# Where ScalarE makes the gate rows of four tokens: one block of eight per group, or two blocks of four in neighbouring places

## The reference, cut to what matters

```python
idx = i1 * PEER_KEYS + i2
gate = jax.nn.softmax(best_s, axis=-1).astype(x.dtype)
...
hid = jnp.einsum('td,tkd->tk', xb, u[ib])
act = jax.nn.gelu(hid, approximate=False) * gb
return jnp.einsum('tk,tkd->td', act, v[ib])
```

## Time and profile before

| | |
|---|---|
| median of 3 runs | 3329.31 us (3320.22 to 3340.08) |
| the profiled execution | 3332.39 us |
| its span, first to last instruction | 3330.6 us |
| TensorE busy with matmuls, share of the span | 99% |
| VectorE, ScalarE, GpSimd busy | 83%, 60%, 14% |
| mean granted clock of TensorE | 0.995 |

### The profile page before, as it was taken

How to read it: one execution, slowest core, us unless ns; L and a number is a source line. 1 busy time by engine, 2 the same in 40 slices (tenths; PEclk the granted TensorE clock), 3 DMA queues, 4 the chain that set the end, 5 groups by cost and what they waited for, 6 DMA issues and landing times. The chain is left out here.

```text
span 3330.6 us, 52168 instructions
## 1 busy us (share of the span) xinstructions
PE 3287.9 (99%) x19468; PEld 2943.0 (88%) x19468; DVE 2780.6 (83%) x4033; ACT 1992.6 (60%) x3618; POOL 482.5 (14%) x262
## 2 busy tenths in 40 slices
PE   9999999999999999999999999999999999999998
PEld 8888879999999988888878887999999998888887
DVE  5775569999988878888987757999898888888988
ACT  4444555555888855555555545555688875555555
POOL 0000000011222211223210000011122211122330
PEclk9999999999999999999999999999999999999999
DMA  7553345798999989999984344578899999999996
GB/s 271 179 185 131 113 160 191 257 347 317 360 360 363 366 336 351 359 360 383 377 307 153 119 152 157 201 285 334 316 377 363 364 341 350 359 354 365 375 378 225
DMA packets 169221, 969.07 MB, mean 291 GB/s; under 512 B 18912, under 2 KB 52704, under 8 KB 55648
## 3 DMA queue, kind: packets, MB, share of 16 engines
q1 hardware_dynamic: 132192, 698.61, 55.7%
q0 software_dynamic: 36864, 268.45, 21.5%
HBM read 951.26 MB, written 15.73 MB: 290 GB/s over the span
## 5 line engine op out<-in xcount | busy, mean ns | idle before, releaser
L1688 DVE TENSOR_TENSOR wl<-raw,wh 128x1024 fp32r<-128x1024 f32 x1264 | 1522.8, 1219 | 421.1 <-ACT wh L580 416.2
L580 ACT ACTIVATE wh<-raw 128x1024 fp32r<-128x1024 f32 x1264 | 1334.0, 1058 | 775.6 <-PE ps L1018 659.2
L1018 PE MATMUL ps<-xx,wh 128*128 128x384 f32 (+1 forms) x5504 | 1707.5, 373 | 9.2 <-DVE wl L1688 4.9
L1018 PE MATMUL ps<-xx,wl 128*128 128x192 f32 (+1 forms) x5504 | 1420.6, 258 | 0.0
L1018 PE MATMUL ps<-wh,act 128*128 128x512 f32 x3584 | 1191.5, 390 | 4.0 <-DVE act L1702 3.9
L1018 PEld LDWEIGHTS ps<-xx,wh 128*128 128x128 f32 x5504 | 1033.9, 188 | 82.7 <-DVE wl L1688 11.1
L1018 PEld LDWEIGHTS ps<-xx,wl 128*128 128x128 f32 x5504 | 1048.2, 190 | 0.5
L1018 PE MATMUL ps<-wl,act 128*128 128x512 f32 x2304 | 897.4, 389 | 0.0
L1018 PEld LDWEIGHTS ps<-wh,act 128*128 128x128 f32 x3584 | 673.8, 188 | 146.8 <-DVE wl L1688 6.6
L1018 PEld LDWEIGHTS ps<-wl,act 128*128 128x128 f32 x2304 | 433.0, 188 | 89.5
L1662 POOL DMA_INDIRECT arena<-in_urows,idx x128 | 209.2, 1634 | 1953.9 <-DVE idx L1948 1131.9
(11 more groups left out here) (217 smaller groups left out, 1567.8 us busy)
## 6 DMA issues: line engine op xcount, KB each, us to landing
raw<-in_u SPq DMA_DIRECT2D x256, 1024.0 KB
raw<-in_v SPq DMA_DIRECT2D x256, 1024.0 KB
raw<-in_w SPq DMA_DIRECT2D x118, 1024.0 KB
h_scratch<-hring SPq DMA_DIRECT2D x128, 96.0 KB
hring<-h_scratch SPq DMA_DIRECT2D x128, 96.0 KB
arena<-in_memT SPq DMA_DIRECT2D x4, 512.0 KB, 7.1
raw<-in_w SPq DMA_DIRECT2D x4, 512.0 KB, 9.1
arena<-in_xT SPq DMA_DIRECT2D x4, 512.0 KB, 8.7
```

The costliest lines, as they stand in the source:

```text
L580: nc.scalar.activation(wh[:, j, :], raw_piece(p), ACT.Copy).then_inc(hi_ready, 1)
L1018: return nc.tensor.matmul(out, lhs, rhs, start=start, stop=stop, **kw)
L1688: v.tensor_tensor(wl[:, j, :], raw_piece(p), wh[:, j, :].bitcast(F32), ALU.subtract).then_inc(lo_ready, 1)
```

## The change

The eight gate rows of a group are made by two calls of four. Each group's halves have a place of their own: in the middle of a slab, between the gelu and the odd piece's `hi` (`ROWS_MID`), or at its end (`ROWS_LAST`). Group 0: middle and end of slab 0. Group 1: middle and end of slab 1. Group 2: end of slab 2, middle of slab 3. Group 3: middle and end of slab 4. Group 4: middle and end of slab 5. Group 5: end of slab 6, middle of slab 7. The number of gate rows, what they compute and the other engines' lists stay as they are.

```diff
-GATE_SLAB = tuple(p // 2 - 1 for p in Q_PIECE)
+ROWS_MID = {0: ((0, 0),), 1: ((1, 0),), 3: ((2, 1),), 4: ((3, 0),), 5: ((4, 0),), 7: ((5, 1),)}
+ROWS_LAST = {0: ((0, 1),), 1: ((1, 1),), 2: ((2, 0),), 4: ((3, 1),), 5: ((4, 1),), 6: ((5, 0),)}
...
-            def gate_rows(q):
+            def gate_rows(q, half):
                 act.wait_ge(onehot_ready, 2 * (q + (layer * QUADS + 1)))
-                for t in range(4):
+                for t in (2 * half, 2 * half + 1):
...
                     gelu(i * slabs + (s - 1), s - 1)
+                    for k, half in ROWS_MID.get(s, ()) if spread else ():
+                        gate_rows((i - SPREAD0) * Q_TRIP + k, half)
                     for n in ahead[-1:]:
                         hi(i * (2 * slabs) + (u0 + n), n % RING)
...
-                    for k in range(Q_TRIP) if spread else ():
-                        if GATE_SLAB[k] == s:
-                            gate_rows((i - SPREAD0) * Q_TRIP + k)
+                    for k, half in ROWS_LAST.get(s, ()) if spread else ():
+                        gate_rows((i - SPREAD0) * Q_TRIP + k, half)
```

## The result

The changed kernel takes **3335.43 us** (median of 22 runs, 3329.15 to 3345.71). The kernel before, run beside it, takes 3326.85 us (22 runs; the 3329.31 shown ahead of the prediction was the median of the first three). The ratio is 1.0026, with a 95% interval of 1.0018 to 1.0033: some 8.6 us slower, where 4.2 us faster was forecast. In a second set of runs it was 1.0031 (1.0023 to 1.0040).

What follows compares the result with a forecast made beforehand. TensorE was taken as the bound, its weight loads leaving 14.1 us open in the spread stages. Trip gains of 1.5 and 2.7 us sum to 4.2, taking the median from 3329.3 to 3325.1 us; range 3312 to 3338.

Steps and rivals of the forecast that it cites:

- The ceiling of 14.1 us: Both spread stages: most that can be won, 655.0 us less the 640.9 covered by TensorE's weight loads.
- stops A, B and C: TensorE waits per trip: A, slab 7's fold, 0.31 us; B, piece 9, 0.20; C, piece 11, 0.17.
- 0.1 and 0.25 new at pieces 14 and 0: Late `lo` stops piece 14 for 0.1 us and, in six-dot trips, the next trip's piece 0 for 0.25.
- Sum: Both stages: ten six-dot trips gain 0.15 us each, six five-dot trips 0.45 each, together 4.2 us.
- Slabs 6 and 7: Group 5's split removes the fold's stop, 0.33 us; VectorE's lateness adds 0.25 at the next piece 0 in six-dot trips.
- DMAs: Slab loads behind `lo` 5 and `lo` 13 start about 1.2 and 0.7 us later; cost taken as 0.
- the first part of the sum: Apparently slabs 0 and 1: four rows ahead of `hi` 5 delay it and `lo` 5 by 1.21 us, cost 0.
- Nothing is won, since the transfers set the pace: Rival: six-dot trips, at 374 GB/s, can't shrink; removed stops return as slab waits; 3329 us, chance 0.20.
- six-dot trips: Trips with six dot products, ten of the 16; each was forecast to gain 0.15 us.
- All stops go: Rival: margins fall right, VectorE catches up and the 14.1 us ceiling is reached; 3315.2 us, chance 0.15.
- Slower: late slab loads: Rival: slab 5's load, 1.2 us later, lands late each trip and `hi` 10 waits; 18 us lost, 3347, chance 0.17.

Runs made afterwards that it cites:

- the best version: Against the kernel before: groups 2 and 5 split in seven trips, group 2 alone in the last; 3312.15 us, 0.9965, and again 3313.82, 0.9964.
- both causes of the loss taken away: Changed kernel with only group 2 split in the last trip and quarter-row gathers, against the kernel before with such gathers: 3319.20 us, 0.9979.
- light gathers: Gathers of `u` cut to a quarter row, except a layer's first two; against the unmodified kernel before: changed kernel 1.0002, kernel before 0.9990.

## Why the prediction was wrong

**What held.** The ceiling of 14.1 us, read from the weight loads and not from the matmuls: the best version gains 12 to 14. The places and causes of stops A, B and C. In the trip, stops A and B gone, C kept, 0.1 and 0.25 new at pieces 14 and 0: found as 0, 0, 0.2, 0.15 and 0.25. The same reckoning, done for other places of the halves, forecast 12 us gained for groups 2 and 5 (11 and 8 measured) and 30 us lost for the other four (32 measured). With both causes of the loss taken away, the stages gain 3.0 us where the sum has 4.2. The reason given for the small gain was the right one: the halves ahead of `hi` 5 and `hi` 13 delay VectorE.

**The step that failed first** is in the **Sum**: "With ten trips of the first kind and six of the second: 1.5 + 2.7 = **4.2 us**". It multiplies one trip by sixteen, and so puts the end of the stage at nothing without a reason. In *Slabs 6 and 7* the four rows behind the gelu "are done with 0.1 to spare before the gate matmuls". They are in time in the last trip of the profiled execution too, but what stands behind them isn't. No slab follows there. Four rows, `hi` 17 and `gates_out` stand ahead of the last side copy, TensorE has nothing else to do, and it waits 0.69 and 0.94 us for 0.43 in all. That is 0.8 to 1.2 us a layer, and a fall of the clock after it costs 1.6 to 3.3 us more (10.6 to 12.2 us in the two ends of the changed kernel, 10.5 to 13.8 in those of its kernel without stores). The mean of the ends went from 9.9 us (8 ends of the kernel before, its light and storeless forms among them) to 12.7 (8 of the changed kernel's), 5.7 us for both layers. The prediction named no rival for it. It had read only the trips.

**The second** is "**DMAs.** [...] I take 0". The slack of the slab loads was looked at, that of the stores was not. The prediction's slower rival named late slab loads; they were found (6 waits for 2 in the first layer), but the store behind them on SyncE's list was waited for longer, 9.7 us against 3.2. A likely reason is in the first part of the sum. `lo` of odd pieces is later, so the slab load starts later: in the second layer's stage 36 of 63 stores follow a load by 1.3 to 1.6 us, where before 43 did by 2.0 to 2.8. But before, 16 followed by 0.4 to 0.7, and none of them was waited for. So ScalarE's slack must play a part: before, it waited up to 1.6 us for TensorE, 24 times in the first stage, and now, with four rows in the middle of a slab, 12 times. No run parts the two.

The stages' gain was forecast at 4.2 us (3.0 came with both causes away). The four stages of the changed kernel's two profiles took 324.3 us on average for 323.1, 2.3 us lost for both, so the transfers cost some 5 to 7 us. That estimate rests on few profiles; light gathers, which bring the stages to 321.3, agree with it. The 2.3 us of the stages and the 5.7 of the ends make 8.0 of the 8.6 us. Which share is the stores' and which the slabs' stays open.

**The rivals.** "Nothing is won, since the transfers set the pace" took the pace for fixed: the best version moves 371 GB/s over whole stages, more than the 361 of before. Its six-dot trips shrink to 40.5 us at up to 380 GB/s, from 41.25 us for the trip of the prediction, and it is 12 to 14 us faster. The Trainium skill's 358 GB/s for one core (DMA: Bandwidth & Descriptors, Where 436 GB/s comes from) is no hard bound here; the measurement decides. "All stops go" was right for another form of the change. "Slower: late slab loads" came in small part: its waits are there, but those for stores are longer and the ends cost more, and neither is in it.

## What to carry to other kernels

Splitting work that stands in the way pays where the second half doesn't fall ahead of what the next engine waits for: two of six places paid here, and the other four took back more than that when they were split alone. After a replay of the steady trip, replay the first and the last one too, since there the work that hid a delay is missing. And of each instruction that moves later ask which transfers it releases, and what queues behind these on the same engine.

## What the runs showed of the hardware

- A wait of TensorE of under 1 us can cost several. With two stops within 4 us, of 0.40 to 0.96 and 0.93 to 1.72 us, the granted clock fell to its lower level for 3.4 or 6.8 us at 10 of 14 ends. With one stop, mostly of 0.34 to 0.48 us, it did at 2 of 22, after stops of 0.65 and 0.89. The waits cost 0.8 to 1.2 us an end at which the clock held, a fall 1.6 to 3.3 more.
- A store of 96 KB that was issued 1.3 us after a load of 1 MB on the same queue, with the DMA engines busy for 0.95 of the time, was waited for until 12 us after its issue.
- The matmul records covered 325.9 of 328 us in a stage in which the weight loads covered 320.8, and what could be won there was what the weight loads left open.
